# Handing every second expert weight load from SyncE's DMA queue to ScalarE's

## The reference

```python
def ec_moe(h, router_w, w_gate, w_up, w_down):
    ...
    gate, idx = lax.top_k(jnp.swapaxes(aff, 1, 2), cap)
    ...
    xg = jnp.take_along_axis(h, flat[..., None], axis=1).reshape(B, N_EXPERTS, cap, D)
    a = jax.nn.silu(jnp.einsum('becd,edf->becf', xg, w_gate)) * jnp.einsum('becd,edf->becf', xg, w_up)
    y = jnp.einsum('becf,efd->becd', a, w_down) * gate[..., None].astype(h.dtype)
    return jnp.zeros_like(h).at[jnp.arange(B)[:, None], flat].add(y.reshape(B, N_EXPERTS * cap, D))
```

## Time and profile before

| | |
|---|---|
| median of 3 runs | 1295.76 us (1294.1 to 1299.89) |
| the profiled execution | 1295.58 us, span 1293.8 us |
| PE / DVE / ACT / POOL busy | 91% / 41% / 31% / 11% of the span |
| moved in all | 296.81 MB |
| begun from SP's queue (q1) / from POOL's (q0) | 284.25 MB / 11.01 MB |
| mean granted clock of TensorE | 0.959 |

### The profile page before, as it was taken

How to read it: one execution, slowest core, us unless ns; L and a number is a source line. 1 busy time by engine, 2 the same in 40 slices (tenths; PEclk the granted TensorE clock), 3 DMA queues, 4 the chain that set the end, 5 groups by cost and what they waited for, 6 DMA issues and landing times.

```text
span 1293.8 us, 24256 instructions
## 1 busy us (share of the span) xinstructions
PE 1181.2 (91%) x10653; PEld 774.8 (60%) x10653; DVE 535.9 (41%) x753; ACT 396.5 (31%) x657; POOL 137.3 (11%) x192
## 2 busy tenths in 40 slices
PE   5789999999998979679899599999999999999994
PEld 3567888888988868569778234444444443333441
DVE  2787334656178787878866501111111110111100
ACT  3313324555467667453411111111111111001111
POOL 1022000121000010100001001111111111111001
PEclk7899999999999999789999699999999999999998
DMA  8620630211323222234743989999999999999992
GB/s 314 230 89 25 203 98 20 93 43 59 98 78 90 76 91 66 83 124 149 246 136 143 350 323 378 386 391 392 391 393 392 392 392 392 391 389 392 401 398 78
DMA packets 111905, 296.81 MB, mean 229 GB/s; under 512 B 7092, under 2 KB 33076, under 8 KB 111800
## 3 DMA queue, kind: packets, MB, share of 16 engines
q1 hardware_dynamic: 108280, 284.25, 58.3%
q0 software_dynamic: 3520, 11.01, 3.7%
HBM read 278.47 MB, written 16.78 MB: 228 GB/s over the span
## 4 chain that ended last, share of the span: by engine, by line
PE 37%; DMA 11%; DVE 3%; ACT 1%; issue 0%; SPq 0%; POOL 0%; DVEq 0%; ACTq 0%; POOLq 0%
PE ps L2027 20%; PE ps L2030 10%; DMA arena<-in_w_exp_up_dram 10%; PE ps L1685 1%; PE ps L1687 1%; PE ps L1686 1%; PE ps L2010 1%; DMA arena<-xn_rows,arena 1%; DVE arena L1311 1%; PE ps L2037 1%; PE ps L1985 1%; PE ps L1972 0%; DMA arena<-in_w_out_dram 0%; SPq L828 0%; DVE w_lo L1187 0%
## 5 line engine op out<-in xcount | busy, mean ns | idle before, releaser
L2027 PE MATMUL ps<-arena 128*32 128x512 f32 x3072 | 402.3, 595 | 6.7 <-ACT arena L1161 2.9
L2030 PEld LDWEIGHTS ps<-arena 128*32 128x32 f32 x3072 | 100.8, 110 | 229.8 <-issue 229.8
L2030 PE MATMUL ps<-arena 128*32 128x256 f32 x3072 | 237.0, 380 | 0.0
L1685 PE MATMUL ps<-act_hi,w_hi 128*128 128x320 f32 x576 | 185.0, 321 | 6.1 <-DVE act_lo L1548 2.6
L1687 PE MATMUL ps<-act_hi,w_lo 128*128 128x320 f32 x576 | 179.7, 312 | 0.0
L1686 PE MATMUL ps<-act_lo,w_hi 128*128 128x320 f32 x576 | 179.6, 312 | 0.0
L2027 PEld LDWEIGHTS ps<-arena 128*32 128x32 f32 x3072 | 95.4, 110 | 77.1 <-issue 6.3
L1685 PE MATMUL ps<-w_hi,act_hi 128*128 128x512 f32 x280 | 112.5, 402 | 11.8 <-DVE w_lo L1187 4.9
L1148 ACT ACTIVATE arena<-ps 64x512 f32<-64x512 f32 x32 | 19.0, 593 | 326.6 <-PE ps L2030 326.4
L1685 PEld LDWEIGHTS ps<-act_hi,w_hi 128*128 128x128 f32 x576 | 110.0, 191 | 9.4 <-DVE act_lo L1548 3.0
L1686 PEld LDWEIGHTS ps<-act_lo,w_hi 128*128 128x128 f32 x576 | 110.0, 191 | 0.0
(11 more groups left out here) (216 smaller groups left out, 1314.2 us busy)
## 6 DMA issues: line engine op xcount, KB each, us to landing
arena<-in_w_exp_gate_dram SPq DMA_DIRECT2D x64, 1024.0 KB
arena<-in_w_exp_up_dram SPq DMA_DIRECT2D x64, 1024.0 KB
arena<-in_w_exp_down_dram SPq DMA_DIRECT2D x64, 1024.0 KB
arena<-in_w_mod_dram SPq DMA_DIRECT2D x23, 1024.0 KB, 5.2
arena<-in_w_in_dram SPq DMA_DIRECT2D x18, 1024.0 KB, 6.1
arena<-in_w_in_dram SPq DMA_DIRECT2D x12, 512.0 KB, 5.6
gl_raw<-arena SPq DMA_DIRECT2D x32, 160.0 KB, 1.8
arena<-gl_raw SPq DMA_DIRECT2D x8, 640.0 KB, 9.9
```

Source lines behind the costliest of these rows:

```text
L1685: t.matmul(out, sh, mh, start=start, stop=False)
L2027: t.matmul(bank(2 * pr)[32 * s:32 * s + 32, :], lat[:, 32 * (s % 2):32 * (s % 2) + 32], w[:, kk, 512 * (s // 2):512 * (s // 2) + 512], sta ...
L2030: ins = t.matmul(bank(2 * pr + 1)[32 * s:32 * s + 32, 0:256], ctx_, w[:, kk, 256 * s:256 * s + 256], start=kt == 0, stop=kt == 7)
```

## The change

`epiece` becomes a function of the issuing engine and holds the wait for the buffer. SP begins pieces 0 to 8 as before and from then on only the even ones. ScalarE begins the odd ones, 92 in number, between its own instructions: `pieces_until(done)` begins all odd pieces whose buffer comes free at or before `done` used pieces, and it stands ahead of each ScalarE instruction that waits for a count of used pieces anyway.

```diff
+        def epiece(eng, n):
+            if n >= NRE:
+                eng.wait_ge(s_eu, n - NRE + 1)
...
+            src = w[ex, 2 * P * k:2 * P * k + 2 * P, :].rearrange("(k p) n -> p k n", p=P)
+            eng.dma_start(eraw[n % NRE].rearrange("p (k n) -> p k n", k=2), src).then_inc(s_er[n % NRE], 16)
...
             for n in range(NRE, NP):
-                sp.wait_ge(s_eu, n - NRE + 1)
-                epiece(n)
+                if n % 2 == 0:
+                    epiece(sp, n)
...
+            odd = [n for n in range(NRE, NP) if n % 2]
+
+            def pieces_until(done):
+                while odd and odd[0] - NRE + 1 <= done:
+                    epiece(act, odd.pop(0))
+
             for e in range(NE):
+                pieces_until(gate_made(e))
                 act.wait_ge(s_eu, gate_made(e))
                 if e:
                     act.wait_ge(s_aT, e)
                 a.activation(aa[:, 0:HW], pair(0)[:, 0:HW], ACT.Silu).then_inc(s_silu, 1)
                 if e:
+                    pieces_until(down_made(e - 1))
                     ycopy(e - 1)
+                else:
+                    pieces_until(10)
                 act.wait_ge(s_aT, e + 1)
                 a.activation(hT, pair(3)[:, 0:HW], ACT.Copy).then_inc(s_ahi, 1)
```

More of the change, by code:

```diff
@@ L717, in crossed @@
             return a[:, :, 0:min(n, row):2, :]
+        wg, wu, wd = (A[n][0] for n in ("w_exp_gate", "w_exp_up", "w_exp_down"))
+        def epiece(eng, n):
+            if n >= NRE:
+                eng.wait_ge(s_eu, n - NRE + 1)
+            if n < 8:
+                w, ex, k = (wg, wu)[n // 4], 0, n % 4
+            elif n >= NP - 4:
+                w, ex, k = wd, NE - 1, n - (NP - 4)
+            else:
+                ex, j = (n - 8) // 12 + 1, (n - 8) % 12
+                w, ex, k = (wg, ex, j) if j < 4 else (wu, ex, j - 4) if j < 8 else (wd, ex - 1, j - 8)
+            src = w[ex, 2 * P * k:2 * P * k + 2 * P, :].rearrange("(k p) n -> p k n", p=P)
+            eng.dma_start(eraw[n % NRE].rearrange("p (k n) -> p k n", k=2), src).then_inc(s_er[n % NRE], 16)
         block = ctx.enter_context(nc.Block())
@@ L815, in _ @@
                 sp.dma_start(xn_rows[LAST[i] * P:LAST[i] * P + P, :], xn2[i % 2]).then_inc(s_xrow[i % 2], 16)
[L817 to L830, removed]
+            epiece(sp, 0)
             sp.wait_ge(s_yrow, 16 * NT)
             for n in range(1, 4):
-                epiece(n)
+                epiece(sp, n)
             load(len(PIECES) - 1)
@@ L836, in _ @@
             filled(sp, ("logits", 1))
-            epiece(4)
+            epiece(sp, 4)
             filled(sp, ("affT", 1))
-            epiece(5)
+            epiece(sp, 5)
             for n, key in enumerate((("mod", 10, 1), ("mod", 11, 0), ("mod", 11, 1))):
                 sp.wait_ge(*used[key])
-                epiece(6 + n)
+                epiece(sp, 6 + n)
             for n in range(NRE, NP):
-                sp.wait_ge(s_eu, n - NRE + 1)
-                epiece(n)
+                if n % 2 == 0:
+                    epiece(sp, n)
             sp.wait_ge(s_scat, 32 * NE)
```

## The result

Over nine runs each the changed kernel has a median of 1301.6 us against 1295.76; the ratio is 1.0032 (95% interval 1.0017 to 1.0047). A repeat on another occasion gave 1299.87 against 1297.48, ratio 1.0025 (1.0010 to 1.0041). The ratios compare means and leave out one slow run of the changed kernel, the profiled one (1434.67 us, TensorE's granted clock 0.80); for this reason the profile shown here is that of the repeat. So the change is slower by 0.25 to 0.32%, 3 to 4 us: inside what the forecast called no change, and inside its range of 1290 to 1308. The forecast's narrower range, 1296.5 to 1299.5, holds neither median.

The account below looks back on a forecast made before the run. The prediction took the DMA engines to bound the experts by a little. It summed 1295.58 + 0 + 0 + 2.0 = 1297.6, on the median 1297.8 us, with a range of 1290 to 1308 and its own case 1296.5 to 1299.5.

Parts of the forecast that it names:

- The bound: In the expert stage the DMA engines set the pace by a little, TensorE being held to them after about 1047 us.
- the stall: TensorE's time lost to late pieces in the last expert rounds, 6.3 to 6.8 us, all that better order or issue could remove.
- the lead: Nine buffers hide DMA's falling behind by 1.2 us a round until about 1047 us; expected to end one or two rounds earlier.
- The other sign: The forecast would be wrong if rounds behind 1047 us took over 34.5 us.
- SyncE's issues, 0 us: After 1050 us SyncE's issues, median 2.5 us, should fall back to 0.37 with two queues, worth 0 us.
- ScalarE's issues, 0 us: 92 issues of 0.37 us on ScalarE, six a round, fit into its idle gaps and add 0 us.
- Turns of a single packet: DMA engines take one 4 KB packet from each queue in turn, so even and odd pieces are served together.
- The lateness, +2.0 us, once: Pieces served together land a half to a whole piece later, once, not per piece: +2.0 us, with ends 1.3 and 2.6.
- The price of a row, no change: A weight row on a DMA engine costs the same with two weight queues as with one: no change.
- Order holds: Rival: an engine drains a piece's rows in one turn, or one queue's lead keeps the order; +0, 1295.8 us, chance 0.15.
- two queues move more: Rival: the weight rate rises from 410 to 416 GB/s, about -5 us, to 1291; chance 0.15.
- Two queues move less: Rival: every row costs more when an engine alternates, 26 us at the price beside additions, to 1322; chance 0.25.

Follow-up runs that it names:

- all_act: The changed kernel with ScalarE beginning all pieces from the tenth on and SyncE none, so one queue again; ratio 0.9997 to the kernel before.
- Blocks of four: The changed kernel with the two queues changing hands every four pieces instead of every piece; ratio 1.0071 to the kernel before.
- halves: The changed kernel with every piece from the tenth on cut in two halves of 128 rows, one begun by SyncE, one by ScalarE; ratio 1.0023.
- light kernels: Kernel before, changed, halves and four-piece blocks, each with most 256-column matmuls left out; ratios to the full kernel before 0.9920, 0.9944, 0.9938, 0.9961.
- without gathers: Light kernel before, light changed and light halves with 13 of 16 gathers left out; medians 1268.0, 1268.7 and 1269.2 us.

## Why the prediction was right, and where not

The direction and the bound were right. That the size came out near +2.0 is partly luck: one term of the sum was too large and another, put at nothing, was too small.

*The bound.* Right. DMA sets the pace, and the stall is a few us; rows that went faster ended it, together with TensorE's rounds of 33.3 us for 32.74. One reading was off: the 33.6 us a round from q1's bytes, given as a sign for the rounds behind the lead, doesn't fit the 34.0 of the chain. The 170 us of that window hold four gathers for five rounds, and a gather takes about 1.7 us of weight time in this kernel (mean of 13). The other sign, rounds over 34.5 us, is missed by the mean of 34.4, but two of the five are 35.1 and 35.2 long; before, one was 34.7.

*SyncE's issues, 0 us.* Right: 2.5 us became 0.37 and nothing came of it. What the prediction cites from the Trainium skill (DMA: Bandwidth & Descriptors, Rules for kernel authors), that spreading transfers over issuing engines saves only issue time, held in this trace: 411 GB/s with two queues, 410 with one.

*ScalarE's issues, 0 us.* Right; `all_act` with twice as many, of 2.4 us each in the median, gave 0.9997.

*Turns of a single packet.* Right for two hardware queues as well: a third each inside a gather (42, 39, 36). The length of a gather tells more. Its 80 rows are five for each engine; turns of one packet at 0.22 us make that some 2.2 us beside one weight queue and 3.3 beside two (an estimate), and 2.40 and 3.44 were measured. The rule of the Trainium skill (the same page, Queues, rings and completion order), read as the prediction did, with a piece's 16 rows in one turn, doesn't fit the equal counts: beside turns of 16 rows, a gather with five for an engine wouldn't get half of the packets (63 of 127). Blocks of four don't decide between the two, since turns of a whole piece would mix their order as well.

*The lateness, +2.0 us, once.* This term of the sum was too large, as far as the traces can tell. Between halves and the changed kernel, which differ in order, they show 1.5 us in the light kernels and 0.7 without gathers, near or under the low end of 1.3, by one execution each. In the full kernels (495.1 and 495.0) nothing of it can be seen; why it vanishes there wasn't settled.

*The price of a row, no change.* This is the step that failed, and it made up for the one above. I compared prices with one weight queue and with two where GpSimd is silent, and there the price is unchanged. I had read 0.249 us for a row inside a gather and set it aside as the gather's own. Over 13 whole gathers of that trace it is 0.22, and it is every row's price while a gather lasts; a second weight queue makes it last longer, since GpSimd's share falls from a half to a third. In the light kernels this is 2.1 us over 12 gathers, in halves and in the changed kernel alike, about 0.17 us a gather, and nothing without gathers. In the full kernel it can't be told apart so cleanly: 157.3 MB of weights took 426.6 us before and 425.1 in `all_act`, 427.6 in the changed kernel and 428.4 in halves, and of the 34.4 us for 34.0 behind the lead it is only a part.

*The rivals.* "Order holds" and "two queues move more" are out. "Two queues move less" was on the right track, but in the three or four us of a gather in each round instead of in every row: some 2 us, not 26.

## What to carry to other kernels

With the DMA engines full, as here, a second issuing queue added no bytes, and an issuing engine held behind a long backlog cost nothing. What the second queue did change is turns: every queue in use took an equal share, packet by packet, so it slowed whatever else ran (a gather 2.40 to 3.44 us) and mixed the order in which pieces landed. Keep pieces that are used in order on one queue, and if they are spread, keep neighbours close (one piece apart cost 0.3%, hardly more than halves with 0.2%; four cost 0.7%). Before a change of a full resource, list what shares it and ask what each sharer's stay becomes.

## What the runs showed of the hardware that was not expected

- Inside a gather of 80 rows from DRAM all queues' 4 KB packets took 0.22 us instead of 0.164, the weights' too; inside an addition to DRAM the weights' didn't (0.173), although the addition's own packets took about 0.33 us (69.5% of 16 us over 34).
- Rows of 8 KB went at 418 to 427 GB/s in three stretches of 6 us where rows of 4 KB went at 410 and 416; from 984 to 990, 349 packets of which 41 are small carried 2.52 MB.
- TensorE's transposes of float32 columns two elements apart took 1.11 us where neighbouring ones took 0.70 (80 rows, eight of them), and 0.92 for 0.81 (128 rows, six).
